# A convolution's taps on four engines: one tile more in ScalarE products, two tiles added up by accumulating DMAs, and 15 taps fewer on TensorE

## The reference

```python
proj = h @ w_in + b_in                        # 1024 -> 3 x 2048
val, glu_gate, z = jnp.split(proj, 3, axis=-1)
u = val * jax.nn.sigmoid(glu_gate)
u = depthwise_causal_conv(u, conv_w) + conv_b # 31 taps, one filter a channel
u = jax.nn.silu(layer_norm(u, norm_g, norm_b))
u = u * jax.nn.silu(z)
return u @ w_out + b_out
```

## Time and profile before

| | |
|---|---|
| median of three runs | 821.14 us (820.45 to 821.9) |
| profiled execution: time, span | 820.67 us, 818.7 us |
| granted TensorE clock | 0.999 |
| TensorE matmul busy | 807.0 us, 99% |
| VectorE busy | 602.9 us, 74% |
| ScalarE busy | 395.5 us, 48% |
| GpSimd busy | 542.3 us, 66% |

### The profile page before, as it was taken

One profiled execution on the slowest core, in us unless ns is written; L12 is line 12 of the kernel. 1 busy time (PEld: TensorE's weight loads), 2 busy tenths in 40 slices (PEclk: granted clock), 3 DMA queues, 4 the chain that ended last, 5 costly groups with the idle time before them and its releaser, 6 DMA issues.

```text
span 818.7 us, 11442 instructions
## 1 busy us (share of the span) xinstructions
PE 807.0 (99%) x3891; PEld 681.3 (83%) x3891; DVE 602.9 (74%) x1026; ACT 395.5 (48%) x711; POOL 542.3 (66%) x335
## 2 busy tenths in 40 slices
PE   8999999999999999999999999999999999999996
PEld 8888888888888887888898788888888888888885
DVE  2699999999999978994833192037788888876217
ACT  4654444455564368622342444256666766664210
POOL 4677999995999954594355438426877776387430
PEclk9999999999999999999999999999999999999999
DMA  6333333330032324444233335115766664663412
GB/s 221 103 103 103 92 88 87 93 104 26 25 105 84 109 79 146 157 160 129 52 107 114 101 102 167 54 41 176 206 200 191 201 199 130 186 205 129 155 52 102
DMA packets 123019, 100.01 MB, mean 122 GB/s; under 512 B 15354, under 2 KB 107616, under 8 KB 122972
## 3 DMA queue, kind: packets, MB, share of 16 engines
q1 hardware_dynamic: 122972, 99.42, 40.4%
HBM read 82.36 MB, written 12.58 MB: 116 GB/s over the span
## 4 chain that ended last, share of the span: by engine, by line
PE 95%; DMA 2%; DVE 1%; ACT 0%; issue 0%; SPq 0%; DVEq 0%
PE bank L1694 91%; DMA x_in<-in_x_dram 1%; PE bank L1999 1%; PE bank L2000 1%; DMA prob_kept<-prob 1%; DMA prob_moved<-prob_kept 0%; PE bank L1873 0%; PE bank L1992 0%; DVE prob L1591 0%; PE bank L1926 0%; PE bank L1990 0%; PE bank L1808 0%; DVE prob L1596 0%; SPq L524 0%; ACT bank L1201 0%
## 5 line engine op out<-in xcount | busy, mean ns | idle before, releaser
L730 POOL TENSOR_TENSOR w_lo<-w_raw,w_hi 128x1024 fp32r<-128x1024 f32 x102 | 252.6, 2485 | 114.1 <-ACT w_hi L927 106.8
L1330 DVE SCALAR_TENSOR_TENSOR bank<-u,conv_w,bank 128x512 f32<-128x512 f32 x357 | 238.6, 747 | 0.5
L1694 PE MATMUL bank<-xt_hi,w_lo 128*128 128x512 f32 (+1 forms) x392 | 151.9, 388 | 0.0
L1694 PE MATMUL bank<-xt_hi,w_hi 128*128 128x512 f32 (+1 forms) x392 | 150.9, 385 | 0.0
L927 ACT ACTIVATE w_hi<-w_raw 128x1024 fp32r<-128x1024 f32 x102 | 106.3, 1054 | 92.2 <-PE bank L1694 29.8
L1694 PE MATMUL bank<-xt_lo,w_hi 128*128 128x512 f32 (+1 forms) x392 | 150.8, 385 | 0.0
L1694 PEld LDWEIGHTS bank<-xt_lo,w_hi 128*128 128x128 f32 x392 | 73.7, 188 | 15.0 <-issue 0.5
L1694 PEld LDWEIGHTS bank<-xt_hi,w_lo 128*128 128x128 f32 x392 | 73.7, 188 | 15.0 <-issue 0.5
L1694 PEld LDWEIGHTS bank<-xt_hi,w_hi 128*128 128x128 f32 x392 | 73.6, 188 | 14.7
L767 POOL TENSOR_TENSOR acc<-acc,tap_product 128x512 f32<-128x512 f32 x60 | 77.8, 1297 | 9.7 <-ACT tap_product L960 4.5
L1694 PE MATMUL bank<-ht_hi,w_lo 128*128 128x512 f32 (+1 forms) x208 | 76.4, 367 | 0.0
(11 more groups left out here) (213 smaller groups left out, 1722.0 us busy)
## 6 DMA issues: line engine op xcount, KB each, us to landing
w_raw<-in_a_w_in_dram SPq DMA_DIRECT2D x48, 512.0 KB, 3.7
w_raw<-in_b_w_in_dram SPq DMA_DIRECT2D x20, 512.0 KB, 3.6
prob_kept<-prob SPq DMA_DIRECT2D x16, 640.0 KB, 3.1
prob_moved<-prob_kept SPq DMA_DIRECT2D x64, 160.0 KB, 3.2
w_raw<-in_a_w_out_dram SPq DMA_DIRECT2D x16, 512.0 KB, 4.0
w_raw<-in_b_w_out_dram SPq DMA_DIRECT2D x16, 512.0 KB, 3.5
bundle_raw<-in_b_w_uq_dram SPq DMA_DIRECT2D x16, 256.0 KB, 4.4
x_in<-in_x_dram SPq DMA_DIRECT2D x4, 512.0 KB, 5.8
```

The lines of the kernel that those rows point to most:

```text
L730: nc.gpsimd.tensor_tensor(w_lo[slot][:], w_raw[raw][:], w_hi[slot][:].bitcast(F32), ALU.subtract).then_inc(w_lo_ready, 1)
L1330: nc.vector.scalar_tensor_tensor(out=inner[:] if k < TAPS - 1 else acc[:, t, :], in0=u[:, t, k:k + SEQ], scalar=conv_w[:, column:column + ...
L1694: last = nc.tensor.matmul(out_ap, a, b, start=(start and n == 0 and m == 0), stop=(stop and n == len(parts) - 1 and m == 2))
```

## The change

- Tiles 4 and 5 become a pair. ScalarE writes both products of a tap into one buffer of 128 x 2 x 512 (`pair_times_u`), and a DMA issued by GpSimd adds the buffer, 512 KB, to the two adjacent tiles of `acc` (`add_pair`, `accum_op`). Each such DMA waits until the one before has landed; tap 0 is written to `acc` directly. So 30 DMAs.
- The shared tiles 3 and 9 become one, tile 8: 30 adds on GpSimd instead of 60.
- TensorE computes taps 0 to 5 of tile 12 instead of 0 to 20, and VectorE its other 25. The groups of matrices are cut anew: only the first (six taps) is used by both tiles, the other four of tile 13 are made early, and TensorE takes the first group of tile 13 last.
- VectorE keeps 11 whole tiles instead of 12. The ten adds of GpSimd's column sum keep their places, the pair's tiles last.
- The buffers move: one pair buffer lies where the tap products were, the other where `cos` and `sin` will be written later.
- The pair's taps stand in both queues as: from tile 7's step on, one between the two chunks and one at its end (18), four in the block of z chunk 0, each ahead of three of the 12 shared taps there, and one behind each of z chunks 0 to 8. The other shared taps: 1, 2, 1, 2, 1, 2 in the steps of tiles 10 to 15, and 2, 2, 1, 1, 1, 1, 1, 1 behind z chunks 0 to 7.

```diff
-        MATRIX_TAPS = (21, TAPS)
-        TAP_GROUPS = tuple(range(a, b) for a, b in zip((0, 5, 10, 15, 21), (5, 10, 15, 21, 31)))
-        SHARED_SLOTS = len(TAP_GROUPS) - 1
-        EARLY_MATRICES = {2: ((0, 0), (0, 1)), 3: ((0, 2), (0, 3)), 4: ((1, SHARED_SLOTS),)}
+        MATRIX_TAPS = (6, TAPS)
+        TAP_GROUPS = tuple(range(a, b) for a, b in zip((0, 6, 12, 18, 24), (6, 12, 18, 24, 31)))
+        SHARED_SLOTS = 1
+        EARLY_MATRICES = {2: ((0, 0), (1, 1)), 3: ((1, 2), (1, 3)), 4: ((1, 4),)}
...
-        SHARED_TILES = (3, 9)
-        VECTOR_TILES = tuple(t for t in range(CT) if t not in MATRIX_TILES and t not in SHARED_TILES)
+        PAIR_TILES, SHARED_TILES = (4, 5), (8,)
+        VECTOR_TILES = tuple(t for t in range(CT) if t not in MATRIX_TILES + SHARED_TILES + PAIR_TILES)
...
-        PAIR_SHARE, MATRIX_SHARE, Z_SHARE = 3, (1, 1, 1, 9), 2
+        PAIRS_BEGIN, PAIRS_EACH, PAIRS_MATRIX = PAIR_TILES[1] + 2, 2, 4
+        SHARE = (1, 2, 1, 2, 1, 2)
+        SHARE_MATRIX, SHARE_Z = 12, (2, 2, 1, 1, 1, 1, 1, 1)
...
+            def add_pair(k):
+
+                if k == 0:
+                    return
+                pool.wait_ge(pair_ready, 2 * (k + 1))
+                wait(pool, pair_added, 16 * (k - 1))
+                nc.gpsimd.dma_start(acc[:, PAIR_TILES[0]:PAIR_TILES[1] + 1, :], pair_product[k % 2][:],
+                                    accum_op=ALU.add).then_inc(pair_added, 16)
...
                     for g in range(SHARED_SLOTS):
                         conv_matrices(1, g)
-                        for n in matrix_taps(g):
-                            add_product(n)
-                for n in z_taps(i):
+                    for m, n in enumerate(share_matrix_taps()):
+                        if m % 3 == 0:
+                            add_pair(pair_matrix_tap(m // 3))
+                        add_product(n)
+                for k in pair_z_taps(i):
+                    add_pair(k)
+                for n in share_z_taps(i):
                     add_product(n)
...
+            def pair_times_u(k):
+
+                if k == 0:
+                    act.wait_ge(u_ready, PAIR_TILES[1] + 1)
+                else:
+                    wait(act, pair_added, 16 * (k - 2))
+                for n, t in enumerate(PAIR_TILES):
+                    tap = conv_w[:, t * TAPS + k:t * TAPS + k + 1]
+                    if k == 0:
+                        nc.scalar.activation(acc[:, t, :], u[:, t, 0:SEQ], ACT.Identity, scale=tap,
+                                             bias=vec[:, V_CONVB + t:V_CONVB + t + 1]).then_inc(pair_ready, 1)
+                    else:
+                        nc.scalar.activation(pair_product[k % 2][:, n, :], u[:, t, k:k + SEQ], ACT.Copy, scale=tap
+                                             ).then_inc(pair_ready, 1)
...
-                groups = TAP_GROUPS[:SHARED_SLOTS] if m == 0 else TAP_GROUPS
-                for g, taps in enumerate(groups):
+                order = list(range(SHARED_SLOTS)) if m == 0 else list(range(SHARED_SLOTS, len(TAP_GROUPS))) + list(
+                    range(SHARED_SLOTS))
+                for g in order:
+                    taps = TAP_GROUPS[g]
```

More of the change, by code:

```diff
@@ L180, in trunk_kernel @@
         conv_w_lo = own("conv_w_lo", [P, CT * TAPS], F32R)
+        cos_at = place[0]
         cos = own("cos", [P, SEQ])
@@ L221, in trunk_kernel @@
         vsum_odd = at("vsum_odd", reg_e, 2 * TILE, [P, SEQ])
-        tap_product = [at(f"tap_product{i}", reg_e, (2 + i) * TILE, [P, SEQ]) for i in range(2)]
+        tap_product = [at(f"tap_product{i}", reg_e, i * TILE, [P, SEQ]) for i in range(2)]
+        pair_product = [at(f"pair_product{i}", base, 0, [P, 2, SEQ])
+                        for i, base in enumerate((reg_e + 4 * 2 * TILE, cos_at))]
         res = at("res", reg_xt, 0, [P, RT, D_MODEL])
@@ L469, in whole_at, with share_taps, share_matrix_taps, share_z_taps @@
             return ends
-        def pair_taps(t):
+        def share_taps(t):
             n = max(0, t - SHARES_BEGIN)
[L474 to L484, removed]
+            return range(sum(SHARE[:n]), sum(SHARE[:n + 1])) if t >= SHARES_BEGIN else range(0)
+        def share_matrix_taps():
+            return range(sum(SHARE), sum(SHARE) + SHARE_MATRIX)
+        def share_z_taps(i):
+            first = sum(SHARE) + SHARE_MATRIX
+            return range(first + sum(SHARE_Z[:i]), first + sum(SHARE_Z[:i + 1]))
+        def pair_taps(t, n):
+            k = PAIRS_EACH * (t - PAIRS_BEGIN) + n
+            return range(k, k + 1) if t >= PAIRS_BEGIN else range(0)
+        def pair_matrix_tap(n):
+            return PAIRS_EACH * (CT - PAIRS_BEGIN) + n
+        def pair_z_taps(i):
+            k = pair_matrix_tap(PAIRS_MATRIX) + i
+            return range(k, min(k + 1, TAPS))
         LOOP_BEGINS, LOOP_ROUNDS = 3, 2
@@ L750, in value_gate @@
                         split_lo(2 * t + w, w, (2 * t + w) % SLOTS)
+                    if w == 0:
+                        for k in pair_taps(t, 0):
+                            add_pair(k)
                 if t > 0:
@@ L811, in sum_tiles @@
                             pool.wait_ge(pe_conv_kept, len(MATRIX_TILES))
+                        elif t in PAIR_TILES:
+                            pool.wait_ge(pair_added, 16 * (TAPS - 1))
                         else:
@@ L941, in value_gate @@
                     split_hi(2 * t + w, w, (2 * t + w) % SLOTS, 16 * (t + 1))
+                    if w == 0:
+                        for k in pair_taps(t, 0):
+                            pair_times_u(k)
                 keep_value_gate(t - 1, (t - 1) % ROUND)
@@ L1056, in _ @@
                         conv_matrices(1, g)
-                        for n in matrix_taps(g):
-                            tap_times_u(n)
                     keep_conv(0)
+                    for m, n in enumerate(share_matrix_taps()):
+                        if m % 3 == 0:
+                            pair_times_u(pair_matrix_tap(m // 3))
+                        tap_times_u(n)
                 if i == 2:
@@ L1781, in convolve @@
                              for k in taps]
-                    last = product(bank[MATRIX_BANK[m]][:], parts, g == 0, g == len(groups) - 1)
+                    last = product(bank[MATRIX_BANK[m]][:], parts, g == order[0], g == order[-1])
                     if m == 0:
```

18 lines of the change are left out of this document (12 added, 6 removed).

## The result

The changed kernel takes 824.79 us (median of 13 runs, 823.3 to 830.04), the kernel before 820.87 (13 runs, 819.47 to 824.21): ratio 1.0048, 95% interval 1.0032 to 1.0064. I had forecast 817.1 with a range of 811 to 826. The time lies in the range, on the wrong side of no change: the kernel became slower. The profiled execution took 825.54 us, its span 823.5 against 818.7.

What follows compares the result with a forecast made beforehand. TensorE was taken as the bound until 314 us, VectorE arriving together with it. Fewer taps (-10.5), waits at early z chunks (+5.1) and at tile 15 (+1.4) summed to -4.0 us: 817.1 us, range 811 to 826.

Steps and rivals of the forecast that it cites:

- C: Start of TensorE's tap matmuls, at 186.54 us in the kernel before; matrix-block times are counted from it.
- TensorE -10.5: Tap matmuls before z: 45 fewer at 0.2328 us each, 10.5 us less for everything that follows.
- VectorE -10.1: VectorE's taps: 366 instead of 382 saves 10.6 us, less 0.5 for more taps standing alone at the end.
- D: Time one DMA issue takes in GpSimd's queue: taken as 1.0 us, ends 0.4 and 1.4.
- L: Time from a pair DMA's issue to its landing: taken as 4.0 us, ends 3.6 and 6.1.
- z1 +4.4, z2 +0.8: TensorE's waits for GpSimd's w_lo before the second and third z chunks: 4.4 and 0.8 us, together 5.1.
- Value stage +1.4: Tiles 11 to 15: GpSimd falls behind tile by tile, so TensorE waits 1.4 us at tile 15.
- g + x against 7.5: Value stage: value-gate product's finish after tile start plus shared adds, at most 7.5 us for the next w_lo in time.
- From z3 on GpSimd needs 2.4 + D + 1.43 = 4.8 per chunk and gains: z from the fourth chunk: w_lo, DMA issue and one add take 4.8 us, so GpSimd catches up with TensorE.
- All 10 column-sum adds keep their places: After z: GpSimd's column-sum adds stay put, the last pair DMA issued three chunks before the sum is read; no cost.
- Rival 2: Waits for landings in GpSimd's queue delay TensorE's weights in value stage and matrix block, deciding from L = 4.7; slower, 0.26.
- Rival 1: DMA issues cost GpSimd next to nothing, the second z chunk is on time, VectorE's 10.1 us give about 811; chance 0.10.

Runs made afterwards that it cites:

- e2: Changed kernel with three pairs and nine shared taps in the matrix block instead of four and twelve, the rest moved into z; 824.2 us, ratio 1.0035 to kernel before.
- e9: Changed kernel with shared adds before the pair DMA in z, pair and shared taps spread anew, six GpSimd column-sum adds instead of ten; 814.32 us, ratio 0.9934.
- e11: As e9, but GpSimd's column-sum adds of a chunk also come before its pair DMA; 813.93 us, ratio 0.9905 to the kernel before.
- e5: Changed kernel with the pair's DMAs as plain copies instead of accumulations; 815.07 us, ratio 0.9931 to the kernel before.
- e7: Changed kernel without the nine pair taps behind z chunks 0 to 8, products and DMAs left out; 813.13 us, ratio 0.9909 to the kernel before.
- e12: As e9, but with ten column-sum adds on GpSimd, as in the changed kernel, instead of six; 819.55 us, ratio 0.9983 to the kernel before.

## Why the prediction was wrong

The sum was -10.5 + 5.1 + 1.4 = -4.0. Measured were -10.45 of taps and +3.5 at z1, and then what the sum did not have: 3.2 at z7 and z9, 4.3 at the mean, 3.4 at the low clock in both places, 0.5 in small steps, and 0.4 from the place of C. Term by term:

- **TensorE -10.5**: right, -10.45. **VectorE -10.1**: right in size; the last tap came 9.6 us earlier with C 0.4 later. **ScalarE off the path**: right in that no wait of TensorE ended with it; GpSimd waited for a pair product once in the matrix block, 2.4 us.
- **D = 1.0**: near. An issue followed by three adds took 5.01 us in the matrix block, where three adds alone take 4.29, so 0.72; ahead of a w_lo it is the whole 0.87 of the record. Both lie inside 0.4 to 1.4. The term of z1, 4.4 at D = 1, is 5D - 0.6, so 3.0 to 3.8 with them.
- **L = 4.0 (3.6 to 6.1), behind D, so 5.0 from the issue's start**: with no weight load beside it the DMA landed 4.4 to 4.8 from the issue's start, so slightly better than taken. In z it was 5.0 in the median, but up to 7.0. One number for L was the mistake, not its size.
- **z1 +4.4, z2 +0.8**: 3.5 and nothing. The mechanism, GpSimd's queue through the matrix block, was right, and e2 and e9 took that wait away by thinning just that stretch.
- **Value stage +1.4**: nothing. TensorE has no wait there; the DMA landed 4.5 to 5.0 us from the issue's start, and the 11.8 us that GpSimd waited there for landings lay in its free time. The rule that I used there, g + x against 7.5, was not tried apart.
- **"From z3 on GpSimd needs 2.4 + D + 1.43 = 4.8 per chunk and gains"**: this is the step that failed. It counts work and no landing. With one pair per chunk the chain can't go faster than landing after landing. From the end of z1's w_lo (221.69) to that of z8's (260.14 + 2.72 = 262.86) GpSimd took 41.2 us; the step gives 6.3 + 6 x 4.8 = 35.1. 7.8 of it were waits for landings; the rest, 33.3, is 1.8 less than the step gives, so the work in it was not underrated. I had put the landing into the value stage, where two pairs stand in a tile of 10.92 us, and left it out of z, where one stands in a chunk of 5.46.
- **"All 10 column-sum adds keep their places"**: they did, and that was wrong too. I never asked when GpSimd gets there. Before, its sum ended at 281.74 and VectorE took it at 285.35: 3.6 us in hand, while everything around was to move up by 10. By my own D, z1's weights at C + 35.7 = 222.2 and 35.1 to z8 give 257.3, and then come 1.0 + 2.73 + 4 x (2.4 + 2.73) = 24.3 of DMA, adds and w_lo: 281.6, and the mean 1.7 later at 283.3. Without any wait in the value stage that is 3.7 us before, not the 5.4 that -10.5 + 5.1 gives. The true end was 288.39, with the landings.
- **The waits' own price**: not in the sum. Matmuls behind the waits at z1 and at the mean ran at half the granted clock and cost 1.7 + 1.7 us. The kernel before had a full clock throughout, so no row of it could price this; the price is 0.427 - 0.228 = 0.2 us per matmul while it lasts.
- **Rival 2, the landing chain**: the right mechanism and the right sign, with 26 in 100. Its place was wrong. I priced it in the value stage and in the matrix block and gave L = 4.7 behind the issue as the point from which it decides, 5.7 from the issue's start with D = 1. Landings of 4.4 to 5.0 from the start are below that, and TensorE lost nothing by them in either. It bound in z, where the trigger is a landing plus the 0.54 us back to the issue above 5.46 us, so a landing above 4.9. That the time still fell into the stated range is no credit to the mechanism: the range reached to 826 for this rival's sake. **Rival 1, the full gain**, would have needed both queues short: e11, at 811.2 us of span against 818.7, comes near it with the same DMAs.
- **"I am wrong if GpSimd stands idle in front of DMA issues, ... or if weight loads land later beside the accumulations"**: the first did it. Of the second one load was seen (the one issued right behind z1's pair DMA took 7.1 us; before 3.9 at most), but TensorE waited for w_lo, whose place behind the waiting issue was late by itself.

*On the pages that the prediction named.* That the add needs a second source read (the Trainium skill, Collectives: The Full Stack, The bandwidth ceiling: the fold count and why AG ≠ RS ≠ AR) agrees with e5: 4.4 us against 2.8 for a copy, and between the first packet's start and the last one's end 2.65 us against 1.4, 1.9 times as long. The first byte at about 1 us (the Trainium skill, DMA: Bandwidth & Descriptors, Latency and other measured facts) compares with the first packet's record here: 1.14 us after the issue for the copy, 1.45 for the accumulation. By the fit of the Trainium skill (DMA: Bandwidth & Descriptors, Anatomy of one DMA — SWDGE (gpsimd) path), 2.0 us and bytes / 436,000, 512 KB would take 3.2 us, an estimate; the copy took 2.8, the accumulation 4.4.

Left open: why the packets of a pair DMA start later beside a weight load, why the x_in load, and with it C, lands up to 2.5 us earlier or later from run to run, and what decides whether slow matmuls follow a wait.

## What to carry to other kernels

Price an edit on every in-order queue up to the point where the queues join again, not only at the first place where one meets the other: here GpSimd had 3.6 us in hand at the join and the others moved up by ten. A chain of DMAs in which each waits for the last has a pace of its own, landing plus issue; set it against the pace of each stage it runs through, and keep its issue away from the event that sets off another queue's load (1.3 us apart was enough here, worth about 3 us in all). And a wait of TensorE can cost more than its length: waits of 3.5 and 4.3 us brought 1.7 us of slow matmuls each, while the one of 2.3 in e7 brought none. The length alone doesn't tell: 1.9 us of idle time at z9 of e12 were followed by eight slow matmuls, 2.7 at z9 of e2 by none.

## What the hardware showed that I had not expected

An accumulating DMA of 512 KB within SBUF, issued by GpSimd, landed 4.4 us after its issue when alone, against 2.8 for the copy; the accumulation of 256 KB took 3.2. It held GpSimd's queue for 0.7 to 0.9 us (record 0.87). The record of the next instruction starts after 0.61, but it and the ones behind it are recorded up to 0.3 us longer, an add 1.6 instead of 1.3 and w_lo 2.70 instead of 2.40, while they overlap by as much; so behind a DMA ends are to be compared, not lengths. Issued within 0.6 us of a weight load of 512 KB on SyncE's queue, the pair DMA took 5.7 to 7.0 us; with 1.3 us or more between them, 4.4 to 5.5. The load took up to 7.1 where the pair DMA was issued just ahead of it. Alone the two take 4.4 and 3.6. Over a stretch with both, the DMA engines were 0.76 busy in the records; with pair DMAs nearly alone (192 to 214 us) they were 0.50 busy at 100 GB/s. After 3.3 us of waiting TensorE's granted clock was 0.57 in the window from 222 to 226 us, with matmuls 0.427 us apart, the lower of its two levels (1.2 and 2.4 GHz), before it rose again.
